# A chunked linear recurrence on one core: the next head's gates, logarithms and sums spread over the current head, and the outputs put into two PSUM banks in turn

## The reference, cut to what matters

```
f = lb + (1 - lb) * sigmoid(z);  k = 1 - f;  g = log f        # per direction
q = silu(q) * 128**-0.5
S_t = diag(f_t) S_{t-1} + k_t v_t^T ,  o_t = S_t^T q_t         # forward, and on the flipped sequence
out = o_forward + flip(o_backward)                             # latent tokens only
```

## Time and profile before

| what | value |
|---|---|
| median of 3 runs | 4288.93 us (4283.05 to 4293.55) |
| the profiled execution's own time | 4288.4 us |
| its span in the trace | 4286.6 us |
| busy shares of the span | PE 89%, PEld 68%, DVE 59%, ACT 45%, POOL 16% |

### The profile page before, as it was taken

How to read it: one execution, slowest core, us unless ns; L and a number is a source line. 1 busy time by engine, 2 the same in 40 slices (tenths; PEclk the granted TensorE clock), 3 DMA queues, 4 the chain that set the end, 5 groups by cost and what they waited for, 6 DMA issues and landing times. The chain is left out here.

```text
span 4286.6 us, 44398 instructions
## 1 busy us (share of the span) xinstructions
PE 3805.5 (89%) x17525; PEld 2913.7 (68%) x17525; DVE 2523.1 (59%) x2685; ACT 1925.1 (45%) x2509; POOL 702.0 (16%) x565
## 2 busy tenths in 40 slices
PE   7999787897577889999999999899888897998988
PEld 2788643344566558877777877678777576786756
DVE  7421164525785788988888887652166534514753
ACT  4411110004655257767676776542166314424641
POOL 0200023310001102211111111420022123201222
PEclk9999988998788899999999999899999898999999
DMA  7322314204004489999999999433420333435123
GB/s 271 116 90 105 98 58 155 81 30 154 24 27 176 175 311 363 383 368 374 371 373 367 373 375 329 158 118 124 144 102 18 127 121 129 128 111 190 50 72 130
DMA packets 395010, 779.13 MB, mean 182 GB/s; under 512 B 26132, under 2 KB 109920, under 8 KB 394417
## 3 DMA queue, kind: packets, MB, share of 16 engines
q1 hardware_dynamic: 378546, 724.65, 47.2%
q0 software_dynamic: 11328, 41.16, 2.9%
q10 hardware_dynamic: 4928, 10.49, 0.7%
HBM read 664.73 MB, written 111.51 MB: 181 GB/s over the span
## 5 line engine op out<-in xcount | busy, mean ns | idle before, releaser
L2590 DVE TENSOR_TENSOR moe_w_low<-shared_z,moe_w_high 128x2048 fp32r<-128x2048 f32 x256 | 594.3, 2366 | 97.4 <-ACT moe_w_high L2543 96.7
L2543 ACT ACTIVATE moe_w_high<-shared_z 128x2048 fp32r<-128x2048 f32 x256 | 477.0, 1914 | 182.7 <-DMA shared_z<-in_exp_w 177.2
L172 PE MATMUL moe_bank<-moe_w_high,moe_xgT_high 128*128 128x512 f32 x1024 | 404.9, 395 | 15.1 <-DVE moe_w_low L2590 10.0
L174 PE MATMUL moe_bank<-moe_w_high,moe_xgT_low 128*128 128x512 f32 x1024 | 400.1, 391 | 0.0
L173 PE MATMUL moe_bank<-moe_w_low,moe_xgT_high 128*128 128x512 f32 x1024 | 399.9, 391 | 0.0
L2590 DVE TENSOR_TENSOR moe_w_low<-moe_w_raw,moe_w_high 128x2048 fp32r<-128x2048 f32 x128 | 287.3, 2286 | 61.6 <-ACT moe_w_high L2543 61.4
L2543 ACT ACTIVATE moe_w_high<-moe_w_raw 128x2048 fp32r<-128x2048 f32 x128 | 238.3, 1910 | 116.1 <-DMA moe_w_raw<-in_exp_w 115.9
L2822 DVE TENSOR_REDUCE layer_att_nb<-layer_att_scores 128x1 f32<-128x1280 f32 (+1 forms) x144 | 196.9, 1369 | 122.2 <-PE layer_att_scores L2728 122.2
L172 PE MATMUL layer_front_bank<-layer_front_w_high,layer_front_hT_high 128*128 128x512 f32 (+1 forms) x608 | 230.6, 379 | 13.4 <-POOL layer_front_hT_low L651 13.4
L172 PEld LDWEIGHTS moe_bank<-moe_w_high,moe_xgT_high 128*128 128x128 f32 x1024 | 192.9, 188 | 61.1 <-DVE moe_w_low L2590 14.7
L174 PE MATMUL layer_front_bank<-layer_front_w_high,layer_front_hT_low 128*128 128x512 f32 (+1 forms) x608 | 224.5, 369 | 0.0
(11 more groups left out here) (484 smaller groups left out, 8554.9 us busy)
## 6 DMA issues: line engine op xcount, KB each, us to landing
shared_z<-in_exp_w SPq DMA_DIRECT2D x128, 2048.0 KB, 10.5
moe_w_raw<-in_exp_w SPq DMA_DIRECT2D x64, 2048.0 KB, 10.3
mods_raw<-in_ada_w SPq DMA_DIRECT2D x12, 2048.0 KB, 9.1
shared_z<-in_w_in SPq DMA_DIRECT2D x48, 512.0 KB, 6.4
first_raw<-in_w_in SPq DMA_DIRECT2D x32, 512.0 KB, 6.8
late_raw<-in_w_mod SPq DMA_DIRECT2D x8, 2048.0 KB, 8.0
proj_t<-front_out SPq DMA_DIRECT2D x48, 256.0 KB
shared_z<-in_w_out SPq DMA_DIRECT2D x12, 1024.0 KB, 6.9
```

The source lines that it names most:

```text
L172: nc.tensor.matmul(out, lhs[0], rhs[0], start=start, stop=False)
L174: return nc.tensor.matmul(out, lhs[1], rhs[0], start=False, stop=stop)
L2543: nc.scalar.activation(hi, x, ACT.Copy).then_inc(high, 1)
L2590: nc.vector.tensor_tensor(lo, x, hi.bitcast(F32), ALU.subtract).then_inc(low, 1)
```

## The change

The instructions on TensorE and VectorE stay the same in number; their order on ScalarE and VectorE is new, and so are four details.

- `forget_gates(h, d)` is split by direction and separated from the query's step (`queries`) and from the logarithms (`forward_logs`, `backward_logs`). It writes sigmoid(-z) into `kh` (free once that head's transposes are done) and not into KX. Head 1's gates stand right ahead of head 0's tiles; those of head h + 2 stand inside the last tiles of head h, direction 0 between `o_copy(h, 6)` and `kt_copy(h + 1, 3)`, direction 1 between `kt_copy(h + 1, 4)` and `o_copy(h, 7)`. SyncE loads z for head h + 2 after the store of tile 5 of head h.
- Outputs use banks 3 and 5 in turn, and `out(n)` waits for copy n - 2. Transposes of heads 1 to 3 all use bank 4.
- The query sides of the levels are numbered first (j = 0 to 6), the key sides after them.
- VectorE's `keys` and `sums` of the next head move up to tiles 2 and 3 of the current head, and everything behind them by as much.

```diff
-            side, l = divmod(j, LEVELS)
-            return side, l, P >> l + 1
+            k, l = divmod(j, LEVELS)
+            return 1 - k, l, P >> l + 1
...
+        def turn_bank(n):
+
+            return 5 if n < NSB and n % 2 else 4
...
+                        if t == UT + 1 and h + 2 < H:
+                            load_z(h + 2)
...
+                def forget_gates(h, d):
+                    c = d * 4 + h
+                    act.wait_ge(core.load[d].sem, core.load[d].at(h + 1))
+                    if h:
+                        act.wait_ge(turned, NSB * (h - 1) + (STEPS - 1) // SB + 1 if d == 0 else NSB * h)
+                    core.act(act, nc.scalar.activation(kh[d][:, :, :], z[d][:, :].rearrange("p (t c) -> p t c", c=P),
+                                                       ACT.Sigmoid, scale=-1.0))
...
-                    nc.scalar.activation(ob[n % 4][:, :], bank[3][:, 0:P], ACT.Copy).then_inc(ocopied, 1)
+                    nc.scalar.activation(ob[n % 4][:, :], bank[3 + 2 * (n % 2)][:, 0:P], ACT.Copy).then_inc(ocopied, 1)
...
+                forget_gates(1, 0)
+                forget_gates(1, 1)
                 for h in range(H):
-                    u, t = 2 * h, 0
-                    for j in range(10):
+                    u, more = 2 * h, h + 1 < H
+                    for j in range(8):
                         level(u + 1, j)
                     o_copy(h, 0)
-                    for j in range(10, NP):
+                    for j in range(8, NP):
                         level(u + 1, j)
                     o_copy(h, 1)
-                    if h + 1 < H:
-                        forget_gates(h + 1)
+                    if more:
+                        queries(h + 1)
+                        forward_logs(h + 1)
                     o_copy(h, 2)
+                    if more:
+                        backward_logs(h + 1)
+                        carried(h + 1)
+                        for j in range(2):
+                            level(u + 2, j)
                     o_copy(h, 3)
...
                     o_copy(h, 4)
                     if more:
-                        for j in range(8, NP):
+                        for j in range(7, 10):
                             level(u + 2, j)
-                        kt_copy(h + 1, 1)
+                        kt_copy(h + 1, 0)
+                        for j in range(10, NP):
+                            level(u + 2, j)
                     o_copy(h, 5)
                     if more:
+                        kt_copy(h + 1, 1)
                         kt_copy(h + 1, 2)
+                    o_copy(h, 6)
+                    if h + 2 < H:
+                        forget_gates(h + 2, 0)
+                    if more:
                         kt_copy(h + 1, 3)
-                    o_copy(h, 6)
-                    if more:
                         kt_copy(h + 1, 4)
+                    if h + 2 < H:
+                        forget_gates(h + 2, 1)
                     o_copy(h, 7)
...
-                    if n:
-                        pe.wait_ge(ocopied, n)
-                    o = bank[3][:, 0:P]
+                    if n >= 2:
+                        pe.wait_ge(ocopied, n - 1)
+                    o = bank[3 + 2 * (n % 2)][:, 0:P]
...
                     pe.wait_ge(rd, LEVELS * (u + 1))
+                    pe.wait_ge(ed, NP * (u + 1))
```

More of the change, by code:

```diff
@@ L1898, in _ @@
                 for h in range(H):
[L1899 to L1909, removed]
@@ L1910, in _ @@
-                    more = h + 1 < H
+                    u, more = 2 * h, h + 1 < H
+                    masks(h, 0, 0)
+                    for j in range(4):
+                        exponents(u + 1, j)
+                    masks(h, 0, 1)
+                    for j in range(4, 8):
+                        exponents(u + 1, j)
+                    masks(h, 1, 0)
+                    for j in range(8, 12):
+                        exponents(u + 1, j)
+                    masks(h, 1, 1)
+                    for j in range(12, NP):
+                        exponents(u + 1, j)
@@ L1911, in _ @@
+                    for j in range(2):
+                        level(u + 1, j)
+                    masks(h, 2, 0)
+                    if more:
+                        keys(h + 1)
+                    for j in range(2, 4):
+                        level(u + 1, j)
+                    masks(h, 2, 1)
+                    for j in range(4, LEVELS):
+                        level(u + 1, j)
                     if more:
                         sums(h + 1, 0)
-                    masks(h, UT, 0)
+                    masks(h, 3, 0)
@@ L1914, in _ @@
                     if more:
                         sums(h + 1, 1)
-                    masks(h, UT, 1)
+                    masks(h, 3, 1)
                     if more:
-                        for j in range(6):
+                        for j in range(2):
                             exponents(u + 2, j)
-                    masks(h, UT + 1, 0)
+                    masks(h, 4, 0)
+                    if more:
+                        for j in range(2, 5):
+                            exponents(u + 2, j)
@@ L1937, in _ @@
                     if more:
                         carry_state(h + 1, 1)
-                        level(u + 2, 5)
-                        level(u + 2, 6)
+                        for j in range(2, 4):
+                            level(u + 2, j)
+                    masks(h, 6, 1)
+                    if more:
                         carry_state(h + 1, 2)
-                    masks(h, UT + 3, 0)
-                    if more:
-                        for j in range(7, 10):
+                        for j in range(4, LEVELS):
@@ L1945, in _ @@
                             level(u + 2, j)
-                    masks(h, UT + 3, 1)
+                    masks(h, 7, 0)
                     if more:
                         carry_state(h + 1, 3)
-                        for j in range(10, NP):
-                            level(u + 2, j)
+                    masks(h, 7, 1)
+                    if more:
                         carry_state(h + 1, 4)
```

89 lines of the change are left out of this document (44 added, 45 removed).

## The result

The changed kernel takes 4296.78 us (median of 20 runs, 4291.38 to 4303.63), the kernel before 4287.75 (20 runs, 4280.12 to 4293.55). The forecast was 4295, range 4272 to 4305. The interval is 7.3 to 13.3 us in time; the forecast difference of 6.6 us lies just under it.

What follows compares the result with a forecast made beforehand. VectorE was the nearest bound, busy about 57.7 us a head period and idle 13.2 to 13.8. Old waits traded for new summed to +6.6 us, 4295 us (chance 0.67); own range 4279 to 4303, widened to 4272 to 4305.

Steps and rivals of the forecast that it cites:

- The sum: Whole stage: 0.2 ahead of head 0, then +7.8, +2.6, -4.5 and +0.5 for heads 0 to 3, +6.6 us.
- the five long waits: VectorE in head 1: mask (4,0) 3.5, carry 0 2.6, carry 1 1.4, carry 3 6.2, next head's first mask 2.7 us.
- the bounds: Higher clock throughout gives 4281 us; products at the lower clock for longer in each second unit give 4304.
- The gates ahead of key batch 3: Heads 0 and 1: key batch 3 stands behind table load and gates direction 0 on ScalarE; carry 3 waits 6.2 us.
- The late turn: End of heads 0 and 1: the next head's first mask waits 2.7 us for output 7's rest and four products.
- Head 1's gates ahead of head 0: Head 0: ScalarE does these gates first, the forward logarithm ends at 23.1, and sums 0 wait 5.0 us more.
- Mask (4,0) and carry 0: Mask waits 3.5 us for products at TensorE's lower clock; carry 0 waits 2.6, key batch 0 standing behind the tenth exponential.
- carry 1: VectorE waits 1.4 us, as key batch 1 stands behind the fourteenth exponential and output copy 5 on ScalarE.
- The wait for the copy and the earlier sums: Two output banks free TensorE from the copy; waits of 4.1 (logarithm), 3.1 (gates) and at the next unit's first mask go.
- the first rival: No wait replaces the old ones: VectorE runs at its 57.7 us of work, three periods of 61, -31 us, 4258; chance 0.20.
- The clock did not stay low in the second unit: Rival: TensorE stays at the lower clock through each head's second unit, 11 us a head, 4329 us; chance 0.13.
- The tables: ScalarE loads 3 more tables at 1.3 us each; by the Trainium skill's 2.66 the sum would be about 4 us more.

Runs made afterwards that it cites:

- the filled pauses: Changed kernel with 26 and 22 idle matmuls added in TensorE's pauses ahead of the halves of output 3, heads 0 to 2; 4294.69 us, ratio 1.0009.
- the last version: The four edits, with direction 0 of later gates ahead of output copy 6, last level product behind last mask, idle matmuls before output 3; 4264.51 us.
- one bank: Changed kernel with all outputs in bank 3 again, each waiting for the copy ahead of it, new orders kept; 4299.43 us, ratio 1.0027.
- the four edits: Changed kernel: both gates behind key batch 4, head 1's direction 0 into ScalarE's pause, key batch 0 behind output copy 4, exponents 0-4 before mask (4,0); 4268.59 us.

## Why the prediction was right

**The sum.** +6.6 us was forecast for the stage; it measured +8.4 between first mask and last copy, and +9.0 in the medians. By terms: head 0 78.5 (78.8 forecast), head 1 74.7 (73.8), head 2 67.9 (67.1), head 3 36.4 (35.9). The sign and the place of each are right. The term that is too small is the sum of VectorE's steps: I added 57.4 us and took nothing for the short gaps between steps. In head 1 the five long waits are 2.89 + 2.71 + 1.38 + 6.40 + 3.07 = 16.5 us, as forecast (16.4), and busy time is 57.43; the missing 0.8 us of the period are such gaps, and heads 0 and 2 have as much. The trace before had them too: 71.19 us less 57.70 busy and 12.67 of waits leaves 0.8. That head 0 came within 0.3 us is partly luck: its waits were 20.1 us for a forecast of 21.4, and the gaps made up for most of that. The 0.2 us ahead of head 0 can't be judged: that first mask starts between 1055.5 and 1061.0 us in the traces of the kernels here. And the bounds were worked out as 4281 and 4304, while the range called the prediction's own was given as 4279 to 4303, with no reason for the difference.

**The gates ahead of key batch 3.** Forecast 6.2, measured 6.40 twice and 0.38 in head 2. The kernel with both gates last shows the cause. The late turn (2.7 forecast, 2.74 and 3.07 measured) follows from it in part: it falls to 2.01 with that edit.

**Head 1's gates ahead of head 0.** Forecast 5.0, measured 4.50, gone when direction 0 moves into the pause.

**Mask (4,0) and carry 0.** 3.5 forecast, 3.53, 2.89 and 3.07 measured; 2.6 forecast, 2.16 and twice 2.71 measured; carry 1, 1.4 forecast, 0.76, 1.38 and 1.47 measured. The 2.16 and the 0.76 are those of head 0, where the state products took 1.52 us behind a pause of 4.21, and 2.08 behind the same pause in heads 1 and 2. That a part of the first is the clock was argued from one pause, with a wait of 1.3 us at the full clock; the filled pauses show 1.39 in the one head in which they fit, and 2.2 us of the period. In the last version the same matmuls bring the three periods down by 1.3, 1.3 and 2.5 us.

**The wait for the copy and the earlier sums.** That output 3 no longer waits for a copy behind gates is worth 9.1 us under the old orders, shown by the two banks alone. The new orders cost 17.5 us against that kernel (257.48 against 239.99). I had not separated the two; the forecast treats them as one trade.

**The rivals.** VectorE did not run at its 57.7 us; it comes near it (61 to 63 a head) only with the chain of edits, so the first rival was a place that can be reached, not the change as made. The clock did not stay low in the second unit: from mask (4,0) to the next head it was 0.86, 0.83 and 0.89, where the kernel before had 0.85 to 0.86. The tables: the activation starts 1.30 us after the load's start in the changed kernel too (1197.02 to 1198.32), no drain beside it, so the larger figure of the Trainium skill (ScalarE: Activation LUTs, What ACT_TABLE_LOAD costs) is not borne out here.

## What to carry to other kernels

An engine that works in order has two costs for a long step: what the step waits for, and who stands behind it. Moving five microseconds of gates out of one queue place moves the wait to whatever short copy now stands behind them; put long steps where the engine already pauses, and behind the short copies that others wait for. Two changes in one, a second buffer and a new order, are worth timing apart: here the buffer alone gains 9 us and the order loses twice as much, until four queue places are mended. Then buffer and order together gain 20 us over the kernel before, 11 of them over the buffer alone.

## What the runs showed of the hardware

TensorE's clock fell behind shorter pauses than the 4.4 us on which I had counted. In head 0 of the changed kernel the second half of an output ran slow after 1.85 us of idleness, 1.46 us where such a half took 1.16 at the full clock, and the state's part behind it 1.06 instead of 0.61; the granted clock was 1.00 in the 9.9 us before and 0.66 in the 2.25 us from there:

```profile
1067.65 1.46 PE L1764 MATMUL hgrn_bank<-hgrn_v,hgrn_masked 128*128 128x128 f32 x8 [1.85 <-DVE hgrn_masked L1913]
1068.90 1.06 PE L1769 MATMUL hgrn_bank<-hgrn_s,hgrn_qh 128*128 128x128 f32 x4
```

The same half one head later, behind nearly the same pause:

```profile
1146.12 1.16 PE L1764 MATMUL hgrn_bank<-hgrn_v,hgrn_masked 128*128 128x128 f32 x8 [1.78 <-DVE hgrn_masked L1913]
```

With the two banks alone it took 1.16 us behind 1.85 us as well. Behind 2.57 us of idleness such a half took 1.53 and 1.20 us in heads 1 and 2 of the changed kernel, 1.16 with one bank and 2.08 with the four edits. So the length of the last pause does not decide it by itself; what does, no run here separates.

And adding work made the stage shorter: 48 matmuls without effect in each of three heads took 5.1 us off the stage.
